# Head norm moved inside the back part of a gated delta-net layer, with tokens on partitions, and the first weight unit of the output product split there

## The reference

```python
def step(state, xs):                       # over chunks of tokens, 16 value heads of 128
    v_new = u_c - einsum('bhck,bhkv->bhcv', w_c, state)
    o = einsum('bhck,bhkv->bhcv', q_c, state) + einsum('bhij,bhjv->bhiv', attn_c, v_new)
    state = state * last_c[..., None, None] + einsum('bhck,bhcv->bhkv', k_c, v_new)
    return state, o
...
o = rms_norm(o, w_norm) * silu(z)          # per head, over its 128 features
return o.reshape(b, t, GDN_V_DIM) @ w_out  # 2048 x 1024
```

## Time and profile before

| | us |
|---|---|
| runs, median of 3 | 2105.94 (2096.75 to 2109.28) |
| profiled execution, its own time | 2099.09 |
| its span | 2097.4 |
| PE busy | 1940.8 (93%) |
| DVE busy | 1048.2 (50%) |
| ACT busy | 860.5 (41%) |
| POOL busy | 168.4 (8%) |

### The profile page before, as it was taken

One profiled execution on the slowest core, in us unless ns is written; L12 is line 12 of the kernel. 1 busy time (PEld: TensorE's weight loads), 2 busy tenths in 40 slices (PEclk: granted clock), 3 DMA queues, 4 the chain that ended last, 5 costly groups with the idle time before them and its releaser, 6 DMA issues. The chain is left out here.

```text
span 2097.4 us, 31661 instructions
## 1 busy us (share of the span) xinstructions
PE 1940.8 (93%) x12868; PEld 1736.3 (83%) x12868; DVE 1048.2 (50%) x1722; ACT 860.5 (41%) x1380; POOL 168.4 (8%) x190
## 2 busy tenths in 40 slices
PE   7999998989869899999989987889999998899988
PEld 6999997889759899999989965668888885787666
DVE  6667667675573433333344156543343337852243
ACT  6557742345572333232324244433333333424342
POOL 0001221022320000000000011000000002000101
PEclk9999998589989999999999999999999999999999
DMA  7223441113253222323223222222222232311100
GB/s 178 89 72 122 121 159 47 34 43 78 65 143 101 65 97 83 99 80 100 80 62 94 91 58 64 81 80 86 96 100 97 83 100 62 120 43 60 41 1 40
DMA packets 205246, 173.91 MB, mean 83 GB/s; under 512 B 41232, under 2 KB 180496, under 8 KB 205128
## 3 DMA queue, kind: packets, MB, share of 16 engines
q1 hardware_dynamic: 205128, 172.25, 27.6%
HBM read 161.40 MB, written 10.83 MB: 82 GB/s over the span
## 5 line engine op out<-in xcount | busy, mean ns | idle before, releaser
L159 DVE TENSOR_TENSOR main_wlo<-raw,main_whi 128x2048 fp32r<-128x2048 f32 x106 | 242.8, 2292 | 414.4 <-ACT main_whi L152 414.3
L152 ACT CAST main_whi<-raw 128x2048 fp32r<-128x2048 f32 x106 | 201.6, 1904 | 524.5 <-PE ps L174 523.2
L174 PE MATMUL ps<-ffn_xhi,main_whi 128*128 128x264 f32 (+1 forms) x768 | 206.5, 323 | 12.9 <-DVE ffn_xlo L506 12.9
L174 PE MATMUL ps<-ffn_xlo,main_whi 128*128 128x264 f32 (+1 forms) x768 | 207.1, 324 | 0.0
L174 PE MATMUL ps<-ffn_xhi,main_wlo 128*128 128x264 f32 (+1 forms) x768 | 206.4, 323 | 0.0
L174 PE MATMUL ps<-ffn_alo,main_whi 128*128 128x264 f32 (+1 forms) x768 | 205.8, 322 | 0.0
L174 PE MATMUL ps<-ffn_ahi,main_wlo 128*128 128x264 f32 (+1 forms) x768 | 205.0, 321 | 0.0
L174 PE MATMUL ps<-ffn_ahi,main_whi 128*128 128x264 f32 (+1 forms) x768 | 204.6, 320 | 0.0
L174 PE MATMUL ps<-gdn_xhi,gdnf_whi 128*128 128x264 f32 x768 | 162.1, 293 | 5.2 <-DVE gdn_xlo L506 4.4
L174 PE MATMUL ps<-gdn_xlo,gdnf_whi 128*128 128x264 f32 x768 | 158.2, 287 | 0.0
L174 PE MATMUL ps<-gdn_xhi,gdnf_wlo 128*128 128x264 f32 x768 | 157.9, 287 | 0.0
(11 more groups left out here) (477 smaller groups left out, 3804.4 us busy)
## 6 DMA issues: line engine op xcount, KB each, us to landing
raw<-in_ff_up_dram SPq DMA_DIRECT2D x32, 1024.0 KB, 5.4
raw<-in_ff_down_dram SPq DMA_DIRECT2D x32, 1024.0 KB, 5.0
raw<-in_gdn_in_dram SPq DMA_DIRECT2D x24, 1024.0 KB, 5.6
raw<-in_w_in_dram SPq DMA_DIRECT2D x14, 1024.0 KB, 5.3
raw<-in_mlstm_in_dram SPq DMA_DIRECT2D x12, 1024.0 KB, 5.3
raw<-in_gdn_out_dram SPq DMA_DIRECT2D x8, 1024.0 KB, 7.2
gdn_v_spilled<-gdnf_o SPq DMA_DIRECT2D x16, 264.0 KB, 2.2
gdn_z_spilled<-gdnf_o SPq DMA_DIRECT2D x16, 264.0 KB, 2.4
```

The lines of the kernel that those rows point to most:

```text
L152: k.nc.scalar.copy(k.whi[:, slot % SPLIT_SLOTS, :], k.raw[:, slot, :]).then_inc(k.hi_done, 1)
L159: eng.tensor_tensor(k.wlo[:, s, :], k.raw[:, slot, :], k.whi[:, s, :].bitcast(F32), ALU.subtract).then_inc(k.lo_done, 1)
L174: mm = pe.matmul(ps[:, b, 0:k.width], w, x[:, half], start=first and n == 0, stop=last and n == 2)
```

## The change

1. In the back part the output product on TensorE has its two operands exchanged, so that tokens, not features, are on the partitions of `ob`. In step t, for unit t-3, ACT squares `ob` into `hs`, DVE sums over the features of each head (`summed`), ACT takes Ln and Exp(-0.5 x) of the 4 values of a token (`root`) and scales `ob` by them into `hs` (`scale`), PE transposes `hs` back into `ob` (`back`), and DVE multiplies by the gain on its way to `wide` (`leave`). `output` of the next unit waits for `leave` (`h_done`) where it waited for the copy.
2. The stage `head_norm` is gone.
3. The split slots of the weights are tensors of their own, and slot 0 is there from the start, so unit 0 of the output product is split in step 20 of the back part, on ACT and DVE. The output product splits only unit 1 itself, and issues its first three z tiles ahead of the weight unit that is still to load.
4. ACT loads the table set with Silu at the end of the back part.

```diff
+            with nc.allow_non_contiguous_dma(reason="128 gains, feature on partitions"):
+                sp.dma_start(gain[:, :], gain_col).then_inc(s.gain_in, 16)
...
                 if u >= 1:
-                    pe.wait_ge(s.o_done, u)
+                    pe.wait_ge(s.h_done, u)
                 for h in range(GRP):
                     if c > 0:
-                        pe.matmul(ob[:, h, 0:n], st[:, GRP * i + h, :], eq[:, i, h, 0:n], start=True, stop=False)
-                    mm = pe.matmul(ob[:, h, 0:n], new[0:n, u % 2, h, :], dt[0:n, i, h, 0:n], start=c == 0, stop=True)
+                        pe.matmul(ob[0:n, h, :], eq[:, i, h, 0:n], st[:, GRP * i + h, :], start=True, stop=False)
+                    mm = pe.matmul(ob[0:n, h, :], dt[0:n, i, h, 0:n], new[0:n, u % 2, h, :], start=c == 0, stop=True)
                 mm.then_inc(s.o_ready, 1)
+            def back(u):
+                c, i = units[u]
+                n = size(c)
+                pe.wait_ge(s.scaled, GRP * (u + 1))
+                for h in range(GRP):
+                    mm = pe.transpose(ob[:, h, 0:n], hs[0:n, h, :], k.ident[0:n, 0:n])
+                mm.then_inc(s.h_turned, 1)
...
                 if real(t + 1):
                     prepare(t + 1)
+                if real(t - 3):
+                    back(t - 3)
                 if level:
                     open6(t)
...
-            def outputs(u):
-                c, i = units[u]
-                n, t = size(c), first_token(c)
+            def square(u):
+                n = size(units[u][0])
                 act.wait_ge(s.o_ready, u + 1)
-                nc.scalar.copy(out[:, :, 2 * i:2 * i + 2, t:t + n],
-                               ob[:, :, 0:n].rearrange("p (q o) n -> p o q n", o=2)).then_inc(s.o_done, 1)
+                if u >= 1:
+                    act.wait_ge(s.h_turned, u)
+                nc.scalar.square(hs[0:n, :, :], ob[0:n, :, :]).then_inc(s.squared, 1)
+            def root(u):
+                n, b = size(units[u][0]), u % 2
+                act.wait_ge(s.summed, u + 1)
+                nc.scalar.activation(var[0:n, b, :], var[0:n, b, :], ACT.Ln, scale=1.0 / CH, bias=k.eps[0:n, :])\
+                    .then_inc(s.log, 1)
+                act.wait_ge(s.log, u + 1)
+                nc.scalar.activation(var[0:n, b, :], var[0:n, b, :], ACT.Exp, scale=-0.5).then_inc(s.inv, 1)
+            def scale(u):
+                n = size(units[u][0])
+                act.wait_ge(s.inv, u + 1)
+                for h in range(GRP):
+                    nc.scalar.activation(hs[0:n, h, :], ob[0:n, h, :], ACT.Copy, scale=var[0:n, u % 2, h:h + 1])\
+                        .then_inc(s.scaled, 1)
...
                 if real(t - 3):
-                    outputs(t - 3)
+                    square(t - 3)
                 if level:
                     copy5(t)
+                if real(t - 3):
+                    root(t - 3)
+                    scale(t - 3)
                 if real(t - 1):
                     news(t - 1)
...
+                if t == nun:
+                    split_hi(k, act, u_out, 0, None)
             slots(step)
+            nc.scalar.preload_act_table_set("silu_and_others")
...
+            def summed(u):
+                n = size(units[u][0])
+                dve.wait_ge(s.squared, u + 1)
+                dve.reduce_sum(var[0:n, u % 2, :].unsqueeze(2), hs[0:n, :, :], AX.X).then_inc(s.summed, 1)
+            def leave(u):
...
+                dve.wait_ge(s.h_turned, u + 1)
+                dve.tensor_scalar(out[:, :, 2 * i:2 * i + 2, t:t + n], ob[:, :, 0:n].rearrange("p (q o) n -> p o q n", o=2),
+                                  gain[:, 0:1], None, ALU.mult).then_inc(s.h_done, 1)
...
                 if real(t - 3):
+                    summed(t - 3)
                     states(t - 3)
...
                 if level:
                     corner5(t)
+                if real(t - 3):
+                    leave(t - 3)
                 second_half(t)
...
+                if t == nun:
+                    split_lo(k, dve, u_out, 0)
```

More of the change, by code:

```diff
@@ L151, in split_hi @@
         act.wait_ge(k.tile_full, used)
-    k.nc.scalar.copy(k.whi[:, slot % SPLIT_SLOTS, :], k.raw[:, slot, :]).then_inc(k.hi_done, 1)
+    k.nc.scalar.copy(k.whi[slot % SPLIT_SLOTS][:, :], k.raw[:, slot, :]).then_inc(k.hi_done, 1)
 def split_lo(k, eng, u, slot):
@@ L202, in unit_tiles @@
     s = slot % SPLIT_SLOTS
[L203 to L204 removed]
+    whi = k.whi[s][:, :].rearrange("p (k n) -> p k n", k=kts)
+    wlo = k.wlo[s][:, :].rearrange("p (k n) -> p k n", k=kts)
     def one(m, kt):
@@ L665, in split_rings, with weight_slot @@
     k.xhi, k.xlo = sb("xhi", [P, KD, T], F32R), sb("xlo", [P, KD, T], F32R)
-def weight_ring(k, name, ctx):
-    sb = lambda nm, shape, dt: ctx.enter_context(k.nc.sbuf_tensor(f"{name}_{nm}", shape, dt))
-    k.whi, k.wlo = sb("whi", [P, SPLIT_SLOTS, UNIT], F32R), sb("wlo", [P, SPLIT_SLOTS, UNIT], F32R)
+def weight_slot(k, name, ctx, slot):
+    sb = lambda nm, shape, dt: ctx.enter_context(k.nc.sbuf_tensor(f"{name}_{nm}{slot}", shape, dt))
+    k.whi[slot], k.wlo[slot] = sb("whi", [P, UNIT], F32R), sb("wlo", [P, UNIT], F32R)
 class ConvSilu:
@@ L744, in dve_end @@
         pass
[L747 to L820, removed]
@@ L1499, in gdn_back @@
         x5, z5, xz6 = sb("x5", [P, GRP, CH]), sb("z5", [P, GRP * 64]), sb("xz6", [P, 2, GRP * 64])
+        hs, var, gain = sb("hs", [P, GRP, CH]), sb("var", [P, 2, GRP]), sb("gain", [P, 1])
         v_in = [k.sem(f"gdns_v{j}") for j in range(VFS)]
@@ L1502, in gdn_back @@
                  "kt_ready", "kt_done", "vt_ready", "v_done", "ks_ready", "r_done", "new_ready", "new_done", "dec_done",
-                 "su_ready", "s_done", "o_ready", "o_done", "x5_ready", "x5_done", "z5_ready", "z5_done", "y5_ready",
+                 "su_ready", "s_done", "o_ready", "gain_in", "squared", "summed", "log", "inv", "scaled", "h_turned", "h_done", "x5_ready", "x5_done", "z5_ready", "z5_done", "y5_ready",
                  "y5_done", "xz6_ready", "xz6_done", "y6_ready", "y6_done", "cut", "stepped", "one", "back")
@@ L1896, in gdn @@
                       tiles, UnitHeads(g, qk), blocks, an)
-        gdn_back(k, g, qk, an, d, tmp, yt, yt0, gdn_out_unit(ins))
+        gdn_back(k, g, qk, an, d, tmp, yt, yt0, ins["gdn_norm"].rearrange("o p -> p o"), gdn_out_unit(ins))
 def gdn_out(k, ins, then):
     qk = k.wide[:, :].rearrange("p (j t) -> p j t", t=T)
-    tile = lambda j: qk[:, bass.ds(j, 1), :].rearrange("p o t -> p (o t)")
-    head_norm(k, "gdn_on", GV, tile, k.ones[:, :], 1.0 / P, lambda g, j: g[:, 0:1],
-              ins["gdn_norm"].rearrange("o p -> p o"))
-    k.loaded = NCH - 1
+    k.loaded, k.split = NCH - 1, 1
     o = lambda kt: qk[:, (kt % 2) * GQ + kt // 2, :]
@@ L1917, in gated_down @@
     n, kts = KD, GV
-    u0, t0, loaded = k.unit, k.tile, k.loaded
+    u0, t0, loaded, split = k.unit, k.tile, k.loaded, k.split
     with ExitStack() as ctx:
@@ L1934, in _ @@
         def _(sp):
-            for u in range(loaded, RAW_SLOTS):
-                load_unit(k, sp, u0 + u, cols(u), ring(u))
             for kt in range(kts):
@@ L1940, in _ @@
                 sp.dma_start(z[:, kt % 3, :], gate_d.ap()[kt]).then_inc(z_in[kt % 3], 16)
+                if kt == 2:
+                    for u in range(loaded, RAW_SLOTS):
+                        load_unit(k, sp, u0 + u, cols(u), ring(u))
             for u in range(RAW_SLOTS, n):
@@ L1946, in _ @@
         def _(act):
-            split_hi(k, act, u0, ring(0), t0)
-            split_hi(k, act, u0 + 1, ring(1), t0)
+            for u in range(split, 2):
+                split_hi(k, act, u0 + u, ring(u), t0)
             for kt in range(kts + 1):
@@ L1966, in _ @@
         def _(dve):
-            split_lo(k, dve, u0, ring(0))
-            split_lo(k, dve, u0 + 1, ring(1))
+            for u in range(split, 2):
+                split_lo(k, dve, u0 + u, ring(u))
             def low(kt):
```

36 lines of the change are left out of this document (21 added, 15 removed).

## The result

| | before | after |
|---|---|---|
| runs, median (range), us | 2102.38 (2093.89 to 2109.28), 6 runs | 2166.62 (2165.44 to 2172.20), 6 runs |
| ratio to before, 95% interval | | 1.032 (1.029 to 1.035) |
| profiled execution, its own time | 2099.09 | 2165.44 |
| span; mean granted clock | 2097.4; 0.957 | 2163.7; 0.937 |

What follows compares the result with a forecast made beforehand. PE was taken to bound the level steps, a loop through ACT, DVE and POOL steps 16 to 22. 65.6 us of work and waits plus 15.9 of clock less 29.3 gave +52.2, 2151.3; with half of 6.9, 2155 us, range 2128 to 2189.

Steps and rivals of the forecast that it cites:

- What the change takes away: Gap from the back part's end to the first weight matmul: 6.7 of 36.0 us stay, gain 29.3 us.
- Table loads that the diff does not show: ACT loads a table ahead of `root`'s Ln and again ahead of its Exp: 40 loads, 1.30 us each, 52 us.
- Level steps: Steps 9 to 15 of the back part: 3.6 us more wait each, 25.2 us, plus 11.9 us of clock.
- Early steps: Steps 3 to 8 of the back part: `decayed` late and `leave` added, 16 us, plus 0.5 for the short chunk.
- steps 16 to 19: Back part steps without level work: later `news` and added `leave`, 2.9 us for two steps, 2.4 for one, 8 us.
- Tail: From weights of unit 19 to the back part's end: serial units of 7.9 us, 15.9 us more, plus 4 of clock.
- The clock holds: Rival: bursts of PE work between waits keep the clock up, 15.9 us less, 2139 us; chance 0.24.
- Lower level throughout: Rival: PE stays at the lower clock through seven level steps, +34 us, 2189 us; chance 0.13.
- No net cost: Rival: the two loads at `root` cost ACT no time, 25 us against 29.3 gained, 2098 us; chance 0.09.
- 0.13 us a load: Load cost in `root` claimed to decide faster or slower, taken as 4 / 40 of 1.30 us.

Runs made afterwards that it cites:

- e3_split_alone: Kernel before, head norm kept, with only unit 0's split in step 20 and the earlier z tiles: 2098.80 us, ratio 1.0006.
- e4_pe_fill: Changed kernel plus idle 128x128 matmuls in each level step, 8 ahead of `back` and 4 ahead of `open6`: 2147.72 us, ratio 1.024.
- e1_one_set: Changed kernel plus one line loading the table set with Ln and Exp at the start of the back part: 2108.44 us, ratio 1.005.
- e6_reorder_loads: Changed kernel, all 40 loads kept, with `news` ahead of `root` and `scale`, `back` behind `open6`, `leave` behind `differ`: 2167.07 us, ratio 1.033.
- e9_loads_alone: Kernel before plus only two table loads on ACT per unit, between z5's copy and `news`, 40 in all: 2130.22 us, ratio 1.015.

## Why the prediction was right

2155 was predicted, 2166.6 came, inside the range and slower than before, as the forecast had it. Against the profiled execution, the sum lay 14.2 low (+52.2 against +66.4). Its errors lie on the same side but for one: the wait of the level steps was 1.5 too high.

- **What the change takes away: right.** 29.3 predicted, 29.26 measured, 6.7 us left of 36.0. But in `e3_split_alone` the split, which saves 3.4 of it, gave 2.6 back in the last steps, because DVE's half stands in the chain there. The sum had 0.3 for that.
- **Table loads that the diff does not show: right.** They are the cause of most of it; without them the ratio is 1.005. Forty of 1283 ns, the activation 0.01 behind each.
- **Level steps: right in the wait, low in the clock.** Predicted were 25.2 of wait and 11.9 of clock. With the clock held (`e4_pe_fill`) the seven steps grow by 23.7, and the fall adds 17.1, 2.4 each for the 1.7 that I took: the earlier trace rows gave a fall of 3.4 us, and these last longer (from 508 past 515 in the step above).
- **Early steps: 16.5 predicted, 19.3 measured**, and **steps 16 to 19: 8, and 10.3.** The chain from weights to `decayed` was placed rightly: `decayed` stands 5.45 behind the end of weights(17), 5.5 predicted. 1.6 of the latter is the step from weights(16) to weights(17), which grew by 4.0 for 2.4. The 2.8 of the early steps is no more than traces of the same code differ by there.
- **Tail: 19.9 with its clock, 23.4 measured.** A unit took 10.2 to 10.5 for 7.9 (the items of the sum add up to 7.8). The largest part of that is `output`, 3.3 us for the 1.7 of the sum, most of it at the lower clock; the transposes took up to 1.11 for 0.60. I allowed 4 us of clock in the whole tail. The norm's own times were right (square 0.60, sum 0.68, Ln 0.30 for 0.21).
- **The rest** of the 14.2, some 1.7, lies behind the first weight matmul.
- **The rivals.** *The clock holds*, 2139: the windows speak against it; `e4_pe_fill` made its condition in the level steps alone, 2147.7. *Lower level throughout*, 2189: the clock is back at 1.00 by the next step's waits (505 in the windows), and their window has 0.84. *No net cost*, 2098: its condition was made in `e1_one_set`, and it gave 2108.4, 0.5% slower than before, not 4 us faster. Its tail (13.2 for 8.1) and its early steps (10.0 for 6.0, the short chunk included) were too cheap; its level steps (4.8 for 7) were not. The claim that 0.13 us a load decides between faster and slower was wrong with it: even free loads don't make this change faster.
- **One chain where there were two.** The prediction charged the loads to `news` and said that the transposes lie inside PE's new wait. `e6_reorder_loads` shows that this second wait carries a step nearly as long, 13.5, by itself. It changes no term of the sum, but it would have made a wrong promise of the obvious remedy.

## What to carry to other kernels

Look in the compiled order for table loads wherever Ln and Exp move into a stage that had no set with both loaded ahead: the diff doesn't show them, and one line that loads the common set ahead was worth 2.7% here. Before moving an operation out of a chain, find what ends next: here PE waited for both ends of the same chain, and a second buffer gave nothing until the order of the instructions around it was changed too. A stage of 26 us that is dissolved into 20 steps is only a gain if each step takes less than 26/20 us more, waits and clock included.

## What the runs showed of the hardware

With PE idle for 2.00 and 1.05 us in a level step, its granted clock fell from 1.00 to 0.50 once in each step (mean 0.84). Twelve matmuls of 128x128 without use, laid into these stretches, kept it at 1.00 and took 17 to 19 us off the kernel. With one wait of 0.59 us a step (`e1_one_set`) it stayed at 1.00; with one of 1.87 (`e6_reorder_loads`) its mean was 0.87. In `e9_loads_alone` one wait of 2.1 us a step for `corner5` gave two steps of 13.0 us for each of 11.4 and a clock of 0.89: behind the wait that ended at 504 the clock stayed at 1.00, behind the next two it fell. Such a pattern shows only in the mean of several steps.
